# High and low words for the first mixer's input, norm 1's rows on VectorE alone, and an earlier place for two panels of w_o

## The reference, cut to what matters

```python
x = layer_norm(x, ln0_g, ln0_b)
h = x * (1.0 + sc_a) + sh_a                      # "ft" in the kernel, features x tokens
proj = h @ w_in                                  # dn_q dn_k dn_v dn_z dn_a dn_b gl_q gl_k gl_v gl_g gl_r
qkv = silu(causal_dwconv(concat[dn_q, dn_k, dn_v], dn_conv))   # 12 chunks of 128 columns, 4 taps
o_dn = gated_delta_rule(l2_norm(q), l2_norm(k), v, log_a, beta)
o_gla = gla_attention(gl_q, gl_k, gl_v, log_alpha)
y = concat[rms_norm(o_dn)*silu(dn_z), rms_norm(o_gla)*silu(gl_g)] @ w_o
x = layer_norm(ALPHA * x + (1.0 + gt_a) * y, ln1_g, ln1_b)
y = conv_ffn(x * (1.0 + sc_f) + sh_f, w_up, ffn_conv, w_down)  # gated feed-forward, 3 taps
```

## Time and profile before

| what | value |
|---|---|
| median of 3 runs | 3069.57 us (3067.78 to 3075.57) |
| the profiled execution's own time | 3069.53 us |
| its span in the trace | 3068.3 us |
| PE busy | 2920.3 us (95%) |
| DVE busy | 1544.4 us (50%) |
| ACT busy | 995.4 us (32%) |
| POOL busy | 771.3 us (25%) |
| first mixer's gqk products begin | 68.67 us |
| twelve chunks of qkv | 186.4 to 431 us |
| gg loop and w_o's start | 758 to 791 us |
| feed-forward's first product | 923.02 us |

### The profile page before, as it was taken

The page is one execution under the profiler, slowest core; times in us unless marked ns, Lnnn a source line. Parts: engine busy times, 40 slices in busy tenths (PEclk is TensorE's granted clock), DMA queues, the critical chain, the costliest instruction groups (busy, mean ns, idle before and its releaser), DMA issues.

```text
span 3068.3 us, 32961 instructions
## 1 busy us (share of the span) xinstructions
PE 2920.3 (95%) x13228; PEld 2191.1 (71%) x13228; DVE 1544.4 (50%) x2433; ACT 995.4 (32%) x1560; POOL 771.3 (25%) x449
## 2 busy tenths in 40 slices
PE   6999999999989999999999999999989999999998
PEld 2444456666637888888887678788757888888886
DVE  7335543333485545546557574776445343333345
ACT  1236632223212222222223760465454222222112
POOL 3101111121235444444442213311010222222221
PEclk9999999999999999999999999999999999999999
DMA  7210012221341211111113212013211111111111
GB/s 256 76 35 21 28 35 62 66 65 45 140 156 38 75 49 48 49 49 49 50 53 92 66 49 85 22 31 111 90 42 35 55 48 49 48 49 49 50 52 57
DMA packets 199766, 193.58 MB, mean 63 GB/s; under 512 B 16167, under 2 KB 147647, under 8 KB 199615
## 3 DMA queue, kind: packets, MB, share of 16 engines
q1 hardware_dynamic: 197984, 187.09, 19.4%
q10 hardware_dynamic: 1631, 4.40, 0.4%
HBM read 175.43 MB, written 13.89 MB: 62 GB/s over the span
## 4 chain that ended last, share of the span: by engine, by line
PE 80%; DVE 9%; ACT 6%; issue 2%; POOL 1%; DMA 1%; SPq 0%; ACTq 0%; DVEq 0%; POOLq 0%
PE bank L1248 59%; PE bank L1275 6%; PE bank L1582 2%; PE bank L1344 1%; PE bank L1385 1%; PE bank L1399 1%; PE bank L1566 1%; DVE ffn_conv L2193 1%; PE bank L1534 1%; PE bank L1350 1%; PE bank L1217 1%; DVE ffn_conv L2189 1%; PE bank L1553 1%; PE bank L1241 1%; PE bank L1601 0%
## 5 line engine op out<-in xcount | busy, mean ns | idle before, releaser
L1248 PE MATMUL bank<-ft_hi,panel_lo 128*128 128x512 f32 x1312 | 468.4, 392 | 4.2 <-POOL panel_lo L2928 4.2
L2928 POOL TENSOR_TENSOR panel_lo<-panel,panelm_hi 128x1024 fp32r<-128x1024 f32 x64 | 153.3, 2395 | 582.1 <-ACT panelm_hi L2500 582.1
L1248 PEld LDWEIGHTS bank<-ft_hi,panel_lo 128*128 128x128 f32 x1312 | 247.4, 189 | 56.6 <-POOL panel_lo L2928 4.4
L1248 PE MATMUL bank<-ft_hi,panel_hi 128*128 128x512 f32 x704 | 275.0, 391 | 4.7 <-POOL panel_lo L2928 4.7
L1275 PE MATMUL bank<-ft,panel 128*128 128x512 f32 x576 | 271.9, 610 | 7.1 <-ACT mod_part L2624 4.7
L1248 PE MATMUL bank<-ft_lo,panel_hi 128*128 128x512 f32 x704 | 274.6, 390 | 0.0
L2189 DVE TENSOR_SCALAR ffn_conv<-ffn_in,ffn_taps 128x512 f32<-128x512 f32 x88 | 113.9, 1294 | 281.5 <-ACT ffn_in L2764 281.5
L2459 DVE TENSOR_TENSOR resid<-resid,bank 128x512 f32<-128x512 f32 x256 | 174.9, 687 | 151.4 <-PE bank L1248 150.6
L2928 POOL TENSOR_TENSOR panel_lo<-panel,panel_hi 128x1024 fp32r<-128x1024 f32 x66 | 157.8, 2399 | 229.5 <-ACT panel_hi L2500 229.5
L1248 PE MATMUL bank<-ftm_hi,panelm_hi 128*128 128x512 f32 x512 | 200.2, 391 | 2.4 <-DVE ftm_lo L1843 2.4
L1248 PE MATMUL bank<-ftm_hi,panel_lo 128*128 128x512 f32 x512 | 199.9, 390 | 0.0
(11 more groups left out here) (478 smaller groups left out, 5800.0 us busy)
## 6 DMA issues: line engine op xcount, KB each, us to landing
panel<-in_w_in SPq DMA_DIRECT2D x52, 512.0 KB, 3.7
panel<-in_w_ada SPq DMA_DIRECT2D x48, 512.0 KB, 3.8
panel<-in_ffn_w_up SPq DMA_DIRECT2D x44, 512.0 KB, 3.7
panel<-in_w_mlp_in SPq DMA_DIRECT2D x32, 512.0 KB, 3.8
panel<-in_w_mlp_out SPq DMA_DIRECT2D x32, 512.0 KB, 3.6
panel<-in_w_o SPq DMA_DIRECT2D x24, 512.0 KB, 3.5
panel<-in_w_out SPq DMA_DIRECT2D x24, 512.0 KB, 3.6
panel<-in_ffn_w_down SPq DMA_DIRECT2D x22, 512.0 KB, 3.6
```

Of the source, the lines that this page charges most:

```text
L1248: m = te.matmul(ps, a, b, start=(start and j == 0), stop=(stop and j == len(pairs) - 1))
L2928: pool.tensor_tensor(lo, k.view(p), hi.bitcast(F32), ALU.subtract).then_inc(*g.new("halved_lo", p))
```

## The change

1. `ft` is split into words. ACT writes the high word (`ft_high`, 8 activations of 128x1024), DVE subtracts it in place, so that the low word stands where `ft` stood (`ft_lower`, 16 subtractions of 128x512). Chunk 0 of gqk still multiplies plainly with `ft`; each half is turned into its low word after that half of chunk 0.
2. Chunks 1 to 3 of gqk, all of gv, and chunks 0 to 7 of qkv become split products. Their 15 panels are rounded by ACT and POOL, with rings of 3, 3 and 2 places for the high words, laid over memory of other tiles. POOL waits for its own result after each.
3. After chunk 7 DVE adds the words together again, `ft_whole`, 16 additions of 128x512. Chunks 8 to 11 and all later users multiply plainly.
4. `ln0_resid` for tiles 4 to 7 moves behind gqk's chunk 0. Norm 0's rows get a place of their own. SP's load of the gate's bias rows waits for `ft_whole`, and that of the second gate matrix for all of `ln0_resid`.
5. Norm 1's bias rows are added by DVE, right behind its multiplication, instead of by POOL. The rows of tiles 4 and 5 move one panel earlier.
6. The first two panels of w_o are created ahead of the gg loop and rounded before its last product.

```diff
+SPLIT_ORDER = (4, 5, 6, 7, 0, 1, 2, 3)
+SPLIT_CHUNKS = 8
+def split_features(k, kk, cols):
+    high, j = (k.ft_high[0], kk) if kk < 4 else (k.ft_high[kk // 2 - 1], kk % 2)
+    return [high[:, j, cols], k.ft_low[:, kk, cols]]
...
+    gqk = [k.panel("gqk", (c,), rows_of(w_in, 0, D, O_GQ + c * P, P), c > 0) for c in range(4)]
     for h in range(HALVES):
         k.banks.take(("rab", h))
         k.unit("rab", h)
-        for n in range(4 * h, 4 * h + 4):
-            k.unit("ln0_resid", n)
-    projections(k, "gqk", w_in, O_GQ, 512)
+    k.unit("ft_high", (4, 5, 6, 7))
+    for n in range(4):
+        k.unit("ln0_resid", n)
+    k.unit("ahead", used=gqk[1])
+    for c in range(4):
+        for h in range(HALVES):
+            k.banks.take(("gqk", c, h))
+            k.unit("project", "gqk", c, h, gqk[c], used=gqk[c], last=("gqk", c, h))
+            if c == 0:
+                if h == 0:
+                    k.unit("ft_high", (0, 1, 2, 3))
+                k.unit("ft_lower", h)
+        if c == 0:
+            for n in range(4, NT):
+                k.unit("ln0_resid", n)
...
-    token_products(k, "gv", w_in, O_GV, (0,), KD)
+    token_products(k, "gv", w_in, O_GV, (0,), KD, split=True)
...
-        dense += piece_steps(k, "qkv", w_in, 0, c, (0, 1, 2, 3), after=((4, "conv_silu"),))
+        after = ((1, "ft_whole"), (4, "conv_silu")) if c == SPLIT_CHUNKS - 1 else ((4, "conv_silu"),)
+        dense += piece_steps(k, "qkv", w_in, 0, c, (0, 1, 2, 3), after=after, split=c < SPLIT_CHUNKS)
...
-    for c in range(4):
-        p = k.panel("gg", (c, 1), rows_of(w_in, 0, D, O_GG + c * P, P), False)
+    gg = [k.panel("gg", (c, 1), rows_of(w_in, 0, D, O_GG + c * P, P), False) for c in range(4)]
+    made = [k.panel("w_o", (0, h, 0), rows_of(d["w_o"][0], 0, 2 * P, h * BANK, BANK), True) for h in range(2)]
+    for c, p in enumerate(gg):
+        if c == 3:
+            k.unit("ahead", used=made[0])
...
-    made = [k.panel("w_o", (0, h, 0), rows_of(d["w_o"][0], 0, 2 * P, h * BANK, BANK), True) for h in range(2)]
-    k.unit("ahead", used=made[0])
...
-        (2, 4): f2[0:1], (2, 5): f2[1:2], (2, 6): f2[2:4],
-        (2, 7): [lambda: norm_start(k, 1, (6, 7)), *a3, *rows((4, 5))]}, split=True, made=made, plain=(1, 2))
+        (2, 4): f2[0:1], (2, 5): f2[1:2], (2, 6): [*f2[2:4], *rows((4, 5))],
+        (2, 7): [lambda: norm_start(k, 1, (6, 7)), *a3]}, split=True, made=made, plain=(1, 2))
...
+    def ft_lower(h):
+        v.wait_ge(*v.filled("gqk", 0, h))
+        for kk in SPLIT_ORDER:
+            v.wait_ge("ft_high", kk)
+            hi, lo = split_features(k, kk, half(h))
+            dve.tensor_tensor(lo, k.ft[:, kk, half(h)], hi.bitcast(F32), ALU.subtract).then_inc(*v.new("ft_lowered", h, kk))
+    def ft_whole(c, h):
+        v.wait_ge(*v.filled("qkv", c, h))
+        for kk in range(KD):
+            hi, lo = split_features(k, kk, half(h))
+            dve.tensor_tensor(k.ft[:, kk, half(h)], lo.bitcast(F32), hi.bitcast(F32), ALU.add).then_inc(
+                *v.new("ft_whole", h, kk))
...
+    def ft_high(chunks):
+        a.wait_ge(*a.filled("ada_col", SC_A, 1))
+        for kk in chunks:
+            for n0 in (0, 4):
+                a.wait_ge(*a.evicted("feat", 0, n0, kk))
+            if kk < 4:
+                a.wait_ge("spilled%d" % (kk % 3), kk)
+            act.activation(split_features(k, kk, slice(0, T))[0], k.ft[:, kk, :], ACT.Copy).then_inc(*a.new("ft_high", kk))
...
     def gate_rows():
+        sp.wait_ge("ft_whole", 1, KD - 1)
...
     def decay_gates():
+        sp.wait_ge("rows_applied", 0, NT - 1)
```

More of the change, by code:

```diff
@@ L177, in token_products @@
             rows = None if scale is None else (scale, h)
-            p = k.panel(stage, (h, k0), rows_of(w, k0 * P, 2 * P, c0 + h * BANK, BANK), False, rows)
+            p = k.panel(stage, (h, k0), rows_of(w, k0 * P, 2 * P, c0 + h * BANK, BANK), split, rows)
             if k0 == 0:
@@ L282, in ada_steps, with piece_steps @@
     return steps
-def piece_steps(k, stage, w, c0, c, ring, after=(), halves=range(HALVES)):
+def piece_steps(k, stage, w, c0, c, ring, after=(), halves=range(HALVES), split=False):
     steps, panel = [], []
@@ L292, in mult @@
                 if not panel:
-                    panel.append(k.panel(stage, (c,), rows_of(w, 0, D, c0 + c * P, P), False))
+                    panel.append(k.panel(stage, (c,), rows_of(w, 0, D, c0 + c * P, P), split))
                 if q == 0:
@@ L871, in memory @@
     top = second
+    k.norm_rows0 = place("norm_rows0", [P, 2, D], at=start + 4 * D * 34 + 256)
+    k.ft_low = place("ft_low", [P, KD, T], F32R, at=start)
+    k.ft_high = [place(f"ft_high{n}", [P, m, T], F32R, at=x)
+                 for n, (m, x) in enumerate(((4, start + 4 * D * 16), (2, late), (2, rows)))]
+    k.high_first = dict(gqk=[place(f"panel_gqk{n}", [P, D], F32R, at=start + 4 * D * (30 + n) + 256) for n in range(3)],
+                        gv=[place(f"panel_gv{n}", [P, D], F32R, at=start + 4 * D * (8 + n)) for n in range(3)],
+                        qkv=[place(f"panel_qkv{n}", [P, D], F32R, at=start + x) for n, x in
+                             enumerate((4 * D * 15, 4 * D * 33 + 256))])
     k.pre = [place(f"conv_in{n}", [P, 3 + T]) for n in range(2)]
@@ L1041, in panel @@
                 high = self.in_ring((4, 5, "more 0", "more 1"))
+            elif stage in FIRST:
+                high = self.in_ring(tuple(f"{stage} {n}" for n in range(len(self.high_first[stage]))))
             elif stage == "w_o":
@@ L1094, in halves_of @@
             high = self.low[self.high_at[p]]
+        elif stage in FIRST:
+            high = self.high_first[stage][int(self.high_at[p].split()[1])]
         elif stage == "w_o":
@@ L1264, in project @@
         ps = free(stage, c, h)
+        if stage == "gqk" and c:
+            for kk in SPLIT_ORDER:
+                pe.wait_ge("ft_lowered", h, kk)
+                m = wide(ps[:], [y[:, kk, :] for y in w], split_features(k, kk, half(h)), kk == SPLIT_ORDER[0],
+                         kk == SPLIT_ORDER[-1])
+            fill(m, stage, c, h)
+            return
         for kk in range(KD):
@@ L1274, in piece @@
         for kk in (2 * q, 2 * q + 1):
-            m = te.matmul(ps[:], w[0][:, kk, :], k.ft[:, kk, half(h)], start=(kk == 0), stop=(kk == KD - 1))
+            split = stage == "qkv" and c < SPLIT_CHUNKS
+            if stage == "qkv" and c == SPLIT_CHUNKS:
+                pe.wait_ge("ft_whole", h, kk)
+            x = split_features(k, kk, half(h)) if split else [k.ft[:, kk, half(h)]]
+            m = wide(ps[:], [y[:, kk, :] for y in w], x, kk == 0, kk == KD - 1)
         if q == 3:
@@ L3156, in norm_rows @@
             row = d[name]
-            sync.dma_start(k.norm_rows[:, n, :], (row[0] if len(row.shape) == 2 else row).partition_broadcast(P)
+            rows = k.norm_rows0 if s == 0 else k.norm_rows
+            sync.dma_start(rows[:, n, :], (row[0] if len(row.shape) == 2 else row).partition_broadcast(P)
                            ).then_inc(*sp.new("rows_loaded", s, n, step=16))
```

53 lines of the change are left out of this document (33 added, 20 removed).

## The result

The changed kernel takes 3051.19 us (median of 4 runs, 3049.2 to 3054.11), the kernel before 3071.24 us (4 runs, 3067.78 to 3075.57). The ratio is 0.9933, 95% interval 0.9921 to 0.9945. So it is faster by 0.67% (0.55 to 0.79), and the forecast of 3050.3 us lies 0.9 us beside the median. The profiled execution took 3054.11 us, its span is 3052.8 us.

A forecast was written before the change was run, and what follows sets the result against it. PE was taken to bound the first mixer up to 186.4 us, then a chain handed between PE, ACT and DVE; 7.2 + 4.1 - 4.1 + 7.5 + 4.5 = 19.2 us from 3069.53 gave 3050.3 us, range 3030 to 3064 (8 in 10).

The forecast's parts named there:

- gqk: In gqk: 48 split products save 0.182 us each, less a 1.5 us wait for low words; +7.2 us.
- gv: In gv: PE waits 5 us for the late third panel, then restarts slowly; +4.1 us, bounds 1.5 to 14.6.
- chunks of qkv: Chunks 0 to 7 of qkv: 12.0 us saved, less roundings, taps, `ft_whole` and restarts; -4.1 us, bounds +19 to -28.
- w_o's start: Before w_o's first product: the 5.10 us gap and 2.4 us of slow clock go; +7.5 us (5 to 8).
- norm 1's rows: Norm 1's bias additions moved from POOL to DVE, feed-forward's start and the stage behind: +4.5 us (-1 to +8).
- The rival in which PE decides: Chunks of qkv: PE still decides, so the stage gives +19 instead of -4.1; 3027 us, chance 0.14.
- ScalarE's roundings: Chunks of qkv: six panels rounded by ACT at 1.04 us, partly on the chain; cost 4 us (0 to 6.3).
- The taps under GpSimd's roundings: Chunks of qkv: POOL's roundings delay DVE's taps by 2.2 us, one time in four; cost 3 us (0 to 13).
- PE's restarts: Chunks of qkv: 1.5 more restarts at PE's lower clock, 2.4 us each; cost 3.6 us (0 to 10).
- w_o's panels do not come sooner: Rival at w_o's start: ACT or the load is late, 7.5 us less gain; 3058 us, chance 0.07.
- slower: Rival in chunks of qkv: each rounded chunk stops PE once, 5.8 us each, stage -39.9 us; 3086 us, chance 0.08.
- The second chain takes more: Rival in chunks of qkv: words hold DVE by the skill's rule, 14.3 instead of 3 us; 3061.6 us, chance 0.16.

The follow-up runs named there:

- panels alone: Kernel before, with only w_o's first two panels laid ahead of the gg loop and rounded behind gg's third chunk; 3063.81 us, ratio 0.9978.

## Why the prediction was right, point by point

The forecast was 3050.3 us, measured 3051.19. Its five terms against the traces:

| term | predicted | measured | from |
|---|---|---|---|
| gqk | +7.2 | +8.5 | 55.13 to 46.63 |
| gv | +4.1 | +6.2 | 62.6 to 171.6 - 115.2 = 56.4 |
| chunks of qkv | -4.1 | -8.7 | 241.7 to 250.4, gv's end to the delta rule's gates |
| w_o's start | +7.5 | +7.6 | panels alone, b |
| norm 1's rows | +4.5 | +3.2 | c + d |

The sum was 19.2, and is 16.8 here; the four lengths of the table give 17.2 (1892.0 to 1874.8), and the medians 20.05 with an interval of 17 to 24, since what lies outside the four lengths scatters. The first three terms together make 7.2 as predicted and 6.0 as measured in one pair of traces (6.6 with the means of the kernels that share the stage). That sum was met by luck: errors of 1.3, 2.1 and -4.6 us nearly cancelled.

- **gqk.** The products' count and price were right (48 x 0.182 = 8.7). The wait of 1.5 us for the low words did not come: VectorE was through in time.
- **gv.** Panel three was forecast ready 34.3 us after gqk's end, and its product starts 149.59 - 115.21 = 34.4 us after it. The mechanism that sets gv's end was right. What I missed is a second wait beside it: the last tiles of the first panel need the banks that hold gate2's second half, and VectorE empties them late in the chain of the gates. The wait for them ended at 132.81 us, and the panel's at 149.59, with some 24 products (16.1 us by 0.68) between the two. PE reached the third panel's place late by the first wait, and so hardly waited there: the bank took the panel's idle time and added none of its own. The 2.4 us that I charged for the slow restart behind the panel weren't paid there, since the wait was only 0.65 us. That is the whole 2.1 us.
- **Chunks of qkv.** The reading that the chain of ScalarE and VectorE decides here, and not PE's 154.6 of 163.6 us, is shown: PE's work in the stretch fell by 15.3 us and the stage grew by 8.7. The rival in which PE decides, 3027 us, is out. PE's share of the stretch is 85%, forecast about 80%. The size was off by 4.6 us. Three of the stage's terms can be set against the chain, and they do not hold the error:
  - ScalarE's roundings: four copies of panels stand on the chain, 4.0 us, as forecast. (The 60% behind the forecast are ScalarE's share of the stretches where the chain has left PE; of the chain from 186.4 to 350 us it is 28%.)
  - The taps under GpSimd's roundings: three on the chain, 2.31, 2.47 and 2.51 us, where the first tap takes 0.97 to 0.99 us in the chain of before: 4.3 us more, forecast 3.
  - `ft_whole`: one half of the features hidden and the other on the chain for 4.81 us, forecast 5.5.

  Behind `ft_whole`, in the same tile, eight PE records take 6.00 us where the next eight take 3.43. With this slow restart the tile lost 4.81 + 2.6 = 7.4 us: the gain over the trace of before, by the start of the scores' product that ends a tile (line 1450, now 1497), was 348.00 - 334.48 = 13.5 us and then 377.80 - 371.67 = 6.1. The rest, 14.8 - 13.5 = 1.3 us, was lost over the chunks ahead of it, where the forecast without `ft_whole` and restarts had 12.0 - 4 - 3 = +5.0. Of that difference of 6.3 us the taps are 1.3. The other 5.0 and the 2.6 of the last tile, 7.6 us, stand against 3.6 us for restarts. So the mis-sized term is the one for PE's restarts (the granted clock is 0.90 in tiles 2 to 5), or the 12.0 us that the shorter products should have brought; how the 4.0 us divide between the two was not separated. The three taps and the next eight records, on the chain that ended last:

```profile
187.45 2.31 DVE mixed L1973
...
250.25 2.47 DVE mixed L1973
...
277.66 2.51 DVE mixed L1973
...
368.24 3.43 PE bank L1284 x8
```

- **w_o's start** went as forecast in each step: two copies on ScalarE, 5.14 us of GpSimd from 774.96, no gap, and the clock at 1.00 behind it.
- **Norm 1's rows.** VectorE took the eight additions in less time than GpSimd's held it back, as forecast (its busy time in the first 60 us of c fell from 47.9 to 46.5 us), and 6.4 us came of it where the place was left alone. I had the early place at 2.6 us of delay, hidden in a wait that goes. In its stead PE waited 6.37 + 2.21 us for `xhat`, with 2.2 us of it for the small step that GpSimd held back, and 3.2 us of the gain went. I had seen that GpSimd's roundings come sooner, and did not ask what of VectorE would then stand beside them.

Of the rivals, "w_o's panels do not come sooner" and "slower" are out. "The second chain takes more" is true in sign (the stage lost 4.6 us more than forecast), but not by its mechanism: the taps under the roundings cost 4.3 us of the chain and not 14.3.

GpSimd holds back VectorE in four kinds of instruction: `xhat` takes 2.77 us in place of 0.77, a tap 1.67 in place of 0.78, the addition of the earlier trace rows 2.87 in place of 0.69, and the step on 128x2 elements 2.35 in place of 0.16. By the Trainium skill, page SBUF — State Buffer, section Who interferes with whom, the two engines share a pair of ports, and whichever takes it first keeps it for a whole instruction. The traces agree: GpSimd's roundings go on at 2.47 us each (7.40 for three) while VectorE's two `xhat` take 5.54.

## What to carry to other kernels

When PE is 95% busy in a stage, follow the chain of waits before pricing a cheaper product: here 20 us of matmul time in seven chunks bought nothing (the tiles without the additions are 2.7 us longer), while one gap of 5 us with its slow restart bought 7.6. When a trace names one releaser for a gap, look for what would have ended just behind it. Two waits side by side have to be taken away together, and each experiment alone shows nearly nothing. When two kernels come out alike and differ in two things, compare them tile by tile. And when an instruction is moved earlier, see what it pushes, and which other engine's work that then meets.

## What was not expected of the hardware

- A plain TENSOR_SCALAR of VectorE with one large input, `xhat`, is slowed by GpSimd's rounding nearly as much as the two-input instructions: 5.54 us for two, against 1.54.
- The loss does not shrink with the instruction: one on 128x2 elements took 2.35 us in place of 0.16, because it started just behind a rounding of 2.47.
- GpSimd needs 11.49 us for eight additions of 128x512 (1.44 us each), VectorE 4.90 (0.61 each).
- PE's granted clock in the chunks fell from 0.98 to 0.92 with 15 us less work in the stretch. In the tile with `ft_whole` it is 0.86. The eight records at 361.37, behind a wait, took 6.00 us; the eight of the earlier trace rows took 3.65. How much of the stage's loss is the clock's was not measured by itself.
